# A two-layer attention trunk on one core: later query turns, an earlier gate release, a norm chain without r, and products that alternate banks

## What is computed

```
# layer 1: latent attention, 16 heads
u = rms_norm(h, ln) @ w_in                  # [q latent 512 | kv latent 512 | rotary key 64 | gate 2048]
q  = rms_norm(c_q,  ln_q)  @ w_q_up         # 16 heads x (128 + 64)
kv = rms_norm(c_kv, ln_kv) @ w_kv_up        # 16 heads x (128 key + 128 value)
q, k = rms_norm(q, g_q), rms_norm(k, g_k)   # per head, then rotary embedding
h = h + (softmax(causal(q k / sqrt(192))) v * silu(gate)) @ w_o
# layer 2: dilated attention, 16 heads x 3 branches (dilation 1, 4, 16)
k, v = rms_norm(rms_norm(h, kv_ln) @ w_k, g_k), rms_norm(h, kv_ln) @ w_v
q, gate = rms_norm(rms_norm(h, b_ln) @ w_q, g_q), rms_norm(h, b_ln) @ w_gate
o = softmax over the banded keys of all three branches together, with ALiBi
h = h + (o * silu(gate)) @ w_o
```

## Time and profile before

| | |
|---|---|
| median of 3 runs | 1463.5 us (1463.33 to 1464.04) |
| profiled execution, its own time | 1464.21 us |
| its span, first to last instruction | 1461.9 us |
| granted TensorE clock, mean | 0.998 |
| PE busy | 1440.6 us, 99% |
| DVE, ACT, POOL busy | 59%, 47%, 11% |
| instructions | 22821, of which 8008 matmuls |

### The profile page before, as it was taken

The page is one execution under the profiler, slowest core; times in us unless marked ns, Lnnn a source line. Parts: engine busy times, 40 slices in busy tenths (PEclk is TensorE's granted clock), DMA queues, the critical chain, the costliest instruction groups (busy, mean ns, idle before and its releaser), DMA issues.

```text
span 1461.9 us, 22821 instructions
## 1 busy us (share of the span) xinstructions
PE 1440.6 (99%) x8008; PEld 1253.7 (86%) x8008; DVE 858.0 (59%) x1249; ACT 690.3 (47%) x988; POOL 157.9 (11%) x108
## 2 busy tenths in 40 slices
PE   8999999999999999999999999999999999999998
PEld 5799899999988888888888888888888888888998
DVE  7666776758955555555555655555554565545553
ACT  4555555544444445444445444544544444454432
POOL 5111111100011001010100200101010020011000
PEclk9999999999999999999999999999999999999999
DMA  8554444355556544654554554565555455456454
GB/s 310 167 159 133 142 136 140 136 176 177 183 198 193 193 148 163 199 168 154 192 176 145 187 190 145 171 199 162 158 187 188 144 174 192 152 173 193 154 167 136
DMA packets 70209, 250.61 MB, mean 171 GB/s; under 512 B 7792, under 2 KB 8176, under 8 KB 70000
## 3 DMA queue, kind: packets, MB, share of 16 engines
q1 hardware_dynamic: 69984, 248.38, 52.0%
q10 hardware_dynamic: 144, 1.05, 0.2%
HBM read 247.30 MB, written 2.10 MB: 171 GB/s over the span
## 4 chain that ended last, share of the span: by engine, by line
PE 94%; DVE 3%; DMA 1%; issue 1%; ACT 1%; POOL 0%; SPq 0%; DVEq 0%; ACTq 0%; POOLq 0%
PE acc L1102 84%; PE turn L1134 3%; PE pv_bank L1146 3%; PE score L1327 2%; DVE xa_lo L731 1%; PE score L1221 1%; PE score L1219 1%; PE turn L1205 0%; DMA res<-in_xT 0%; PE og_bank L1154 0%; DMA raw<-in_w_in 0%; DVE w_lo L716 0%; DVE xa_hi L728 0%; DVE gate L831 0%; ACT probT L497 0%
## 5 line engine op out<-in xcount | busy, mean ns | idle before, releaser
L716 DVE TENSOR_TENSOR w_lo<-raw,w_hi 128x1024 fp32r<-128x1024 f32 (+1 forms) x458 | 575.8, 1269 | 421.2 <-ACT w_hi L464 420.4
L464 ACT ACTIVATE w_hi<-raw 128x1024 fp32r<-128x1024 f32 x464 | 484.4, 1051 | 331.5 <-PE acc L1102 313.1
L1102 PE MATMUL acc<-w_hi,xa_hi 128*128 128x512 f32 (+1 forms) x1088 | 407.4, 374 | 7.2 <-POOL w_lo L385 4.9
L1102 PE MATMUL acc<-w_hi,xa_lo 128*128 128x512 f32 (+1 forms) x1088 | 398.2, 366 | 0.0
L1102 PE MATMUL acc<-w_lo,xa_hi 128*128 128x512 f32 (+1 forms) x1088 | 397.5, 365 | 0.0
L1102 PE MATMUL acc<-w_hi,xb_hi 128*128 128x512 f32 (+1 forms) x640 | 250.6, 392 | 2.7 <-DVE gate L835 1.8
L1102 PE MATMUL acc<-w_hi,xb_lo 128*128 128x512 f32 (+1 forms) x640 | 246.1, 385 | 0.0
L1102 PE MATMUL acc<-w_lo,xb_hi 128*128 128x512 f32 (+1 forms) x640 | 245.8, 384 | 0.0
L1102 PEld LDWEIGHTS acc<-w_hi,xa_hi 128*128 128x128 f32 x1088 | 205.9, 189 | 42.8 <-issue 10.0
L1102 PEld LDWEIGHTS acc<-w_hi,xa_lo 128*128 128x128 f32 x1088 | 205.6, 189 | 33.5
L1102 PEld LDWEIGHTS acc<-w_lo,xa_hi 128*128 128x128 f32 x1088 | 206.1, 189 | 30.7
(11 more groups left out here) (136 smaller groups left out, 1027.2 us busy)
## 6 DMA issues: line engine op xcount, KB each, us to landing
raw<-in_w_b SPq DMA_DIRECT2D x320, 512.0 KB, 3.4
raw<-in_w_gate SPq DMA_DIRECT2D x32, 512.0 KB, 3.4
raw<-in_w_out_a SPq DMA_DIRECT2D x32, 512.0 KB, 3.4
raw<-in_w_out_b SPq DMA_DIRECT2D x32, 512.0 KB, 3.6
raw<-in_w_kv SPq DMA_DIRECT2D x16, 512.0 KB, 3.5
raw<-in_w_in SPq DMA_DIRECT2D x15, 512.0 KB, 6.2
raw<-in_w_q SPq DMA_DIRECT2D x16, 384.0 KB, 3.0
out_T<-res SPq DMA_DIRECT2D x8, 256.0 KB, 4.1
```

The lines of the kernel that those rows point to most:

```text
L464: nc.scalar.activation(w[0][:, s, 0:width], raw[:, s, 0:width], ACT.Copy).then_inc(hi_ready, 1)
L716: nc.vector.tensor_tensor(w[1][:, s, 0:width], raw[:, s, 0:width], w[0][:, s, 0:width].bitcast(F32), ALU.subtract).then_inc(lo_ready[0], 1)
L1102: last = nc.tensor.matmul(out, x(a), y(b), start=start and k == 0, stop=stop and k == 2, **more)
```

## The change

It has four parts.

1. The turns of the first two query groups of a B pair move from quarters 6 and 7 to quarters 7 and 8, on PE and on ACT.
2. PE's waits for `gate_done` before it takes an accumulator become waits for `gate_step`. DVE's own wait for `gate_done` before it uses the gate stays.
3. In the norm chains r is taken out: with y the unscaled accumulator, r y / sqrt(mean((r y)^2) + EPS) equals y / sqrt(mean(y^2) + EPS / r^2), and EPS / r^2 is `x_eps`, two columns which DVE computes once per stage. ACT squares both token tiles in one instruction, DVE adds `x_eps` with one `scalar_tensor_tensor`, and POOL's multiplication and the semaphore `pool_step` go.
4. `project` no longer calls `three`: for each chunk it issues the first product for both token tiles, then the second for both, then the third, so that each matmul writes another bank than the one before it. The output projections still use `three`.

```
 # POOL
-                nc.gpsimd.tensor_tensor(root[:, 0:width], ms[:, 0:width], mhalf[:, 0:width], ALU.pow)\
-                    .then_inc(pool_step, 1)
-                pool.wait_ge(pool_step, c + 1 if times_r == "in" else c - (B_CHAIN_0 - 3))
-                u = width // TILES
-                nc.gpsimd.tensor_tensor(rms[:, 0:width].rearrange("p (t u) -> p t u", t=TILES),
...
-                                        ALU.mult).then_inc(rms_ready, 1)
+                nc.gpsimd.tensor_tensor(rms[:, 0:width], ms[:, 0:width], mhalf[:, 0:width], ALU.pow)\
+                    .then_inc(rms_ready, 1)
 # ACT
-                if by_tile:
-                    for t in range(TILES):
-                        last = nc.scalar.activation(rows[:, buf, t, 0:width], acc[:, pair, t, 0:width], ACT.Square,
-                                                    scale=r[:, t:t + 1])
-                else:
-                    last = nc.scalar.activation(rows[:, buf, :, 0:width], acc[:, pair, :, 0:width], ACT.Square)
-                last.then_inc(squares, 1)
+                nc.scalar.activation(rows[:, buf, :, 0:width], acc[:, pair, :, 0:width], ACT.Square)\
+                    .then_inc(squares, 1)
...
-                    if s in (6, 7):
-                        g = s - 6
+                    if s in (7, 8):
+                        g = s - 7
                         turned(b_round(i, 5 + g), qT[:, g * 512:g * 512 + 512], 512, q_gain[:, g:g + 1])
 # DVE
                 nc.vector.tensor_scalar(x_ms[:], tok_sum[:], 1.0 / D, EPS, ALU.mult, ALU.add).then_inc(x_mean, 1)
+                nc.vector.tensor_scalar(x_eps[:], tok_sum[:], EPS / D, EPS * EPS, ALU.mult, ALU.add).then_inc(x_scaled, 1)
...
                 dve.wait_ge(sums, c + 1)
-                nc.vector.tensor_scalar(ms[:, 0:n], ss[:, 0, 0:n], 1.0 / span, EPS, ALU.mult, ALU.add)\
-                    .then_inc(means, 1)
+                dve.wait_ge(x_scaled, g + 1)
+                nc.vector.scalar_tensor_tensor(
+                    out=ms[:, 0:n].rearrange("p (t u) -> p t u", t=TILES),
+                    in0=ss[:, 0, 0:n].rearrange("p (t u) -> p t u", t=TILES), scalar=1.0 / span,
+                    in1=x_eps[:].rearrange("p (t u) -> p t u", u=1).broadcast_to([P, TILES, units]),
+                    op0=ALU.mult, op1=ALU.add).then_inc(means, 1)
 # PE
-                        for t in range(TILES):
-                            last = three(acc[:, pair, t, 0:width],
-                                         lambda a: x[a][:, chunk_0 + m * chunks + k, t * P:(t + 1) * P],
-                                         lambda b: w[b][:, slot, k * width:(k + 1) * width],
-                                         start and first, stop and final)
+                        for part, (a, b) in enumerate(((0, 0), (0, 1), (1, 0))):
+                            for t in range(TILES):
+                                last = nc.tensor.matmul(acc[:, pair, t, 0:width],
+                                                        x[a][:, chunk_0 + m * chunks + k, t * P:(t + 1) * P],
+                                                        w[b][:, slot, k * width:(k + 1) * width],
+                                                        start=start and first and part == 0,
+                                                        stop=stop and final and part == 2)
...
-                            pe.wait_ge(gate_done, i)
+                            pe.wait_ge(gate_step, i)
...
-            out_projection(OUT_A_0, OUT_A_FILL_0, [[(gate_done, PAIRS)], [(rows_ready, B_CHAIN_0)]], 0, 0, mla_last)
+            out_projection(OUT_A_0, OUT_A_FILL_0, [[(gate_step, PAIRS)], [(rows_ready, B_CHAIN_0)]], 0, 0, mla_last)
...
-                    if s in (6, 7):
-                        b_turn(i, 0, b_round(i, s - 1), 2 * (s - 6))
+                    if s in (7, 8):
+                        b_turn(i, 0, b_round(i, s - 2), 2 * (s - 7))
```

More of the change, by code:

```diff
@@ L178, in build_program @@
         ms = sb("ms", [P, 8])
-        root = sb("root", [P, 8])
         rms = sb("rms", [P, 8])
         x_ms = sb("x_ms", [P, TILES])
+        x_eps = sb("x_eps", [P, TILES])
         tok_ss = sb("tok_ss", [P, 2 * TILES])
@@ L390, in stream_rms, with chain @@
                 nc.gpsimd.tensor_tensor(r[:], x_ms[:], mhalf[:, 0:TILES], ALU.pow).then_inc(r_ready, 1)
-            def chain(c, width, times_r):
+            def chain(c, width):
                 pool.wait_ge(means, c + 1)
[L395 to L398, removed]
-                nc.gpsimd.tensor_tensor(root[:, 0:width], ms[:, 0:width], mhalf[:, 0:width], ALU.pow)\
-                    .then_inc(pool_step, 1)
-                pool.wait_ge(pool_step, c + 1 if times_r == "in" else c - (B_CHAIN_0 - 3))
-                u = width // TILES
-                nc.gpsimd.tensor_tensor(rms[:, 0:width].rearrange("p (t u) -> p t u", t=TILES),
-                                        root[:, 0:width].rearrange("p (t u) -> p t u", t=TILES),
-                                        r[:].rearrange("p (t u) -> p t u", u=1).broadcast_to([P, TILES, u]),
-                                        ALU.mult).then_inc(rms_ready, 1)
+                nc.gpsimd.tensor_tensor(rms[:, 0:width], ms[:, 0:width], mhalf[:, 0:width], ALU.pow)\
+                    .then_inc(rms_ready, 1)
             lows(1, 1)
@@ L413, in _ @@
                     stream_rms(0)
-                    chain(0, TILES, "in")
+                    chain(0, TILES)
                 if n == 15:
-                    chain(1, TILES, "in")
+                    chain(1, TILES)
                 if n + 4 < LOW_0 and n % 2:
@@ L434, in b_pair @@
                         if s == at:
-                            chain(i * 4 + (B_CHAIN_0 + k), units * TILES, "b")
+                            chain(i * 4 + (B_CHAIN_0 + k), units * TILES)
                     if attend and s == 13:
@@ L670, in b_pair @@
                         n, pair = b_fill(i, par, K01)
[L671 removed]
+                        chain_squares(i * 4 + (B_CHAIN_0 + 1), 1, n, pair, 512)
                     if s in (9, 10):
@@ L774, in stream_mean, with chain_sums @@
                 last.then_inc(x_mean, 1)
-            def chain_sums(c, buf, units, span):
+                for t in range(TILES):
+                    last = nc.vector.tensor_scalar(x_eps[:, t:t + 1], x_sum[t], EPS / D, EPS * EPS, ALU.mult, ALU.add)
+                last.then_inc(x_scaled, 1)
+            def chain_sums(c, buf, units, span, g):
                 dve.wait_ge(squares, c + 1)
@@ L1366, in accumulator_read @@
                     pe.wait_ge(rows_ready, rows)
-                    pe.wait_ge(gate_done, i + PAIRS)
+                    pe.wait_ge(gate_step, i + PAIRS)
                 elif f in (Q01, K01):
@@ L1412, in _ @@
                            [[(v_act, 3 * PAIRS), (v_dve, PAIRS)],
-                            [(rows_ready, B_CHAIN_0 + 4 * PAIRS), (gate_done, 2 * PAIRS)]],
+                            [(rows_ready, B_CHAIN_0 + 4 * PAIRS), (gate_step, 2 * PAIRS)]],
                            OUT_FILLS, B_UNIT_0, b_last)
```

29 lines of the change are left out of this document (15 added, 14 removed).

## The result

Five runs of each kernel on one chip: 1455.79 us after the change (1454.48 to 1456.71) against 1463.6 before (1463.33 to 1466.39). The medians lie 7.8 us apart. The ratio of the runs is 0.9942, with an interval from 0.9929 to 0.9956, which is 6.4 to 10.4 us faster. The profiled execution took 1456.7 us, 0.9 above the median. Its span is 1454.9 us, and the mean granted clock 0.999.

A forecast was written before the change was run, and what follows sets the result against it. PE, busy 1440.6 of 1461.9 us, was taken to bound the kernel by what it issues and waits for. Gains of 6.4 + 0.4 + 1.0 + 0 = 7.8 us gave a forecast of 1456.0 us, range 1452.5 to 1460.0.

The forecast's parts named there:

- D: B pairs: query turns stall in the new place, ACT's late copy holding up weights; 6.4 us lost again, 1462.4; chance 0.06.
- The sign: MLA pairs 2 to 7: idle time before the gate fill's first weight load grows by about 0.4 us.
- C: MLA pairs: the gate's saved wait passes through to the time; 2.8 us more gained, 1453.2; chance 0.06.
- Both halves: Start-up norm chains of the first and second latent: each moves PE's work 0.5 us earlier.
- The left-over at the second turn: Start-up: PE's wait before the second latent's turn falls from 0.58 us to 0.1.
- PE's wait at step 11: Start-up, first latent: PE's wait for the low half falls from 1.81 us to 1.3.
- bounds of 8 us: Projections: a bank change costs 0 to 2.4 ns, 0 to 8.3 us in all; 0 was taken.
- E: PE's clock falls to its 1.2 GHz level; each relapse costs 2.7 us, four make it slower; chance 0.01.

The follow-up runs named there:

- query_chain: Changed kernel with each MLA pair's query norm chain put forward, 1454.25 us; the same with the waits for gate_done put back, 1456.76 us.
- turns_only: Kernel before with only the first two query turns of a B pair moved to quarters 7 and 8: 1457.62 us, ratio 0.9954.
- alternate_only: Kernel before with only the product order changed, each projection matmul writing another bank than the one before: 1464.0 us, ratio 1.0001.
- gate_only: Kernel before with only gate_step for gate_done in PE's waits: 1463.8 us, ratio 0.9998.
- after: The changed kernel with all four parts, against the kernel before: 1455.79 us, ratio 0.9942.
- after_again: The changed kernel run once more, unaltered, beside the kernel before: 1455.68 us, ratio 0.9945.
- grouped: Changed kernel with a whole weight step's products made for token tile 0, then for tile 1: 1455.55 us, ratio 0.9945.

## Why the prediction was right

**As a whole** it gave 1456.0 for 1455.8, and its sum of 7.8 us is what was measured. The mechanism of each term held. That the sum came out to the tenth is luck: part 1 was 0.6 us too large, and 0.5 us was gained where no term stood. In the traces the terms come to 5.8 + 0.3 + 1.0 + 0 = 7.1 us, and 0.5 us more lie outside the span (part 3).

**Part 1, the turns: right in mechanism, 0.6 us too large.** Predicted 6.4, measured 6.25 in time (interval 4.7 to 8.6) and 5.81 in the B stage without its loop gaps. By quarters, in pairs 1 to 6: s=6 falls from 8.28 to 6.93 us, by 1.35, which is the turn's 0.44 and the stall's 0.91 as worked out; s=8 rises by 0.44, which is the turn. The term left out that s=4, s=7 and s=9 take 0.02 to 0.03 us longer each, 0.07 a pair. Where that comes from was not tested. D would have shown longer quarters 8 to 10; beyond the turn's 0.44 us they grow by 0.02, and PE lists no new wait there.

**Part 2, the gate: right.** Predicted 0.4 us at output A and nothing in pairs 2 to 7. The pairs' period stays at 28.45 us while the wait at their start vanishes; the idle time before the gate fill's load grows by 0.39 us in pair 2. The sign asked for this in all of pairs 2 to 7; in pair 4 it fails and in pair 6 it is weak, because the pause at the loop's end, which the wait for the gate had covered, takes the room. The period there doesn't shrink either, so this doesn't speak for C. The start of output A comes 0.28 us earlier, not 0.38: two transposes and their signalling leave 0.32 us where I reckoned with 0.22. In time the part is too small to be measured (0.07 us faster; by the interval, from 1.6 faster to 1.0 slower). C is refuted for this kernel. That the eaten wait was worth 2.5 us where DVE's chain comes first is shown by the two query_chain kernels.

**Part 3, the norm chain: right, in mechanism and size.** From the start of the first latent's squares to the first MLA projection it is 28.33 to 28.38 us in the four traces with the old start-up, and 27.32 to 27.35 in the eight with the new: 1.02 us, predicted 1.0. Both halves show. From those squares to step 11's low half it was 3.71 us in the kernel before and is 3.20 now. From the last projection matmul before the second latent's turn to that turn it is 0.85 or 0.86 us in all four old traces, and 0.34 in all eight new. Both are 0.51 us, predicted 0.5. The left-over at the second turn is some 0.23 us, not 0.1, because the wait was longer than the 0.58 that the row shows. The merged square takes 1.03 us (estimated 0.98), and `scalar_tensor_tensor` 0.16, no more than the 0.17 of `tensor_scalar` (I took 0.03 off). PE's wait at step 11 can't be held to its 1.3 us in one trace: PE reaches that step at another time in each, and in the changed kernel's trace waited 0.30 us.

In time this part alone gave 1.5 us (0.6 to 3.2). The other 0.5 us lies outside the span. An execution's time was 2.20 to 2.34 us longer than its span in every execution without this part (the kernel before, turns_only, alternate_only, gate_only), and 1.75 to 1.85 us in every one with it. Both the profiled executions show it: 1464.2 - 1461.9 = 2.3 us, and 1456.7 - 1454.9 = 1.8. The prediction put this at nothing by taking times and spans as one. What in the shorter program makes it was not tested.

**Part 4, alternation: right.** Zero, and no longer by bounds of 8 us, but to 0.03 us over the B stage. The Trainium skill's TensorE: Matmul & The Clock Gate (Back-to-back issue gap) puts an isolated warm matmul of 512 columns at about 216 ns, and a sustained stream in which each has its weight load at about 131 ns. These traces show neither in any order of the banks: 16.36 us for 72 is 227 ns, with a change each time, every third time or every sixth. E didn't happen either: the clock stands at 1.00 through the 920 us, with a change at each matmul.

## What to carry to other kernels

When PE is near 99% busy, price an edit by the wait that ends last behind it, and then ask for the next wait in the same loop. A period that doesn't move while a wait vanishes tells that another chain sets it, and kernels that cross "that chain earlier" with "this wait gone" tell how much each is worth (here the vanished wait was worth nothing measurable alone, and 2.5 us with the chain earlier). Work put off on an in-order engine is put ahead of something else: name what, and price it, before moving it. A bank that another engine still has to read out is a wait if PE wants it at once, and was none here a quarter later. The order in which matmuls visit their accumulators was free here. And half a microsecond of this change lies in the times and not in the spans: a sum over the trace can't see it.

## What the runs showed of the hardware

**A fixed cost for each matmul.** Matmuls with a weight load each start 226.8 ns apart at 512 columns (43.55 us for 192) and 120.2 ns at 256 (5.77 us for 48), whatever the order. Over 512 and 256 columns at 2.4 GHz (213.3 and 106.7 ns) that is some 13.5 ns each, at both widths and with every order of the banks. What it is made of stays open; no kernel here left a weight load out.

**The end of a loop costs PE time.** At the two loop ends in the B stage PE pauses with no semaphore in the way, and the trace gives "issue" as the cause. The one near 868 us, in the kernel before and in alternate_only:

```profile
867.78 0.49 PE L1102 MATMUL acc<-w_hi,xb_hi 128*128 128x512 f32 x1 [0.86 <-issue]
```

```profile
867.95 0.72 PE L1115 MATMUL acc<-w_hi,xb_hi 128*128 128x512 f32 x2 [1.13 <-issue]
```

In the changed kernel it was 0.25 us in one trace and 0.71 in the other. The sum of the two, by the starts of the matmuls, differed from 0.7 to 2.4 us from trace to trace, with no visible relation to the change. Why a loop's end costs this stays open. It makes a comparison of two spans blind to anything under 1 us, which is why the B stage was compared without it.

**The same start-up differs by 0.9 us.** Five traces whose kernels have the same start-up (after, after_again and the three with DVE's chains moved) reach the first MLA projection between 67.2 and 68.1 us. From the first latent's squares on they agree to 0.02 us, so all of it arises before. The squares stand on ACT behind `r_half`, which waits for r, and r is made behind a weight step whose high half waits for its DMA: that high half started at 36.30 us in after_again and at 35.14 in grouped, the earliest of all (66.0 us). But grouped has another order of products there, so its lead may be more than chance.
